# One decoder step on one core: the samples' delta rule moves into the prompt's block, its state products go between the half levels of the inverses, and its outputs are normed by token

## The reference, cut to what matters

```python
def step(S, xs):                      # per head; for a sample: one chunk of 8 tokens, S from the input
    v_new = u_c - w_c @ S             # u, w come from the inverse of (I + A), A strictly lower triangular
    o = (q_c * exp(gc_c)) @ S + att_c @ v_new
    S = S * exp(g_last) + (k_c * exp(g_last - gc_c)).T @ v_new
...
o = o * rsqrt(mean(o * o, -1) + RMS_EPS) * norm_g * silu(z)
y = o.reshape(B, L, H_DN * DV) @ w_out
```

## Time and profile before

| | |
|---|---|
| Median of 3 executions | 1855.16 us (1853.79 to 1858.89) |
| Profiled execution: time, span of its instructions | 1858.92 us, 1857.1 us |
| Last prompt chunk, from its first matmul to the first of the samples' block | 379.01 to 404.37 us |
| Samples' block, from its first matmul to the first of the next block | 404.37 to 469.92 us |
| TensorE busy, share of the span | 96% |

### The profile page before, as it was taken

The page is one execution under the profiler, slowest core; times in us unless marked ns, Lnnn a source line. Parts: engine busy times, 40 slices in busy tenths (PEclk is TensorE's granted clock), DMA queues, the critical chain, the costliest instruction groups (busy, mean ns, idle before and its releaser), DMA issues. The chain is left out here.

```text
span 1857.1 us, 22145 instructions
## 1 busy us (share of the span) xinstructions
PE 1787.9 (96%) x7791; PEld 1389.3 (75%) x7791; DVE 1153.9 (62%) x2240; ACT 454.9 (24%) x1084; POOL 279.5 (15%) x569
## 2 busy tenths in 40 slices
PE   7999999999889999999999999999899999999999
PEld 5677678997557777777777777777577777777767
DVE  3756578885776676666334665556777666653365
ACT  1433413552132222221002311111322222200041
POOL 0111102645141000000112000002310000001120
PEclk9999999997999999999999999999899999999999
DMA  4222211021212222224113032220122222322211
GB/s 167 68 69 68 64 35 46 1 99 60 92 46 69 71 88 68 81 78 146 68 58 113 1 126 88 80 81 4 63 70 84 76 80 80 108 103 94 80 48 51
DMA packets 44318, 138.05 MB, mean 74 GB/s; under 512 B 4776, under 2 KB 12072, under 8 KB 44080
## 3 DMA queue, kind: packets, MB, share of 16 engines
q1 hardware_dynamic: 41504, 132.90, 21.6%
q10 hardware_dynamic: 2704, 3.74, 0.6%
HBM read 128.32 MB, written 8.29 MB: 74 GB/s over the span
## 5 line engine op out<-in xcount | busy, mean ns | idle before, releaser
L267 PE MATMUL bank<-z,ring 128*128 128x288 f32 x1952 | 512.0, 410 | 7.0 <-DVE z L365 2.9
L267 PEld LDWEIGHTS bank<-z,ring 128*128 128x128 f32 x1952 | 373.6, 192 | 115.2 <-issue 3.2
L267 PE MATMUL bank<-x,ring 128*128 128x288 f32 x1632 | 432.3, 412 | 10.3 <-DMA x<-in_x 6.3
L267 PEld LDWEIGHTS bank<-x,ring 128*128 128x128 f32 x1632 | 313.8, 193 | 103.5 <-issue 13.4
L267 PE MATMUL bank<-y,ring 128*128 128x288 f32 x616 | 160.7, 413 | 5.9 <-DVE x L1692 3.7
L1943 DVE SCALAR_TENSOR_TENSOR scratch<-scratch 128x592 f32<-128x592 f32 x176 | 146.3, 832 | 25.6 <-ACT scratch L1887 24.0
L267 PEld LDWEIGHTS bank<-y,ring 128*128 128x128 f32 x616 | 118.3, 193 | 41.8 <-issue 5.5
L267 PE MATMUL bank<-big,ring 128*128 128x288 f32 x536 | 137.7, 412 | 7.2 <-issue 5.0
L267 PEld LDWEIGHTS bank<-big,ring 128*128 128x128 f32 x536 | 103.1, 193 | 38.6 <-issue 10.2
L1977 POOL COPY scratch<-scratch 128x2 f32<-128x2 f32 x88 | 26.6, 302 | 465.7 <-ACT scratch L1873 465.7
L1887 ACT ACTIVATE scratch<-scratch 128x592 f32<-128x592 f32 x88 | 69.4, 789 | 90.9 <-DVE scratch L1917 89.3
(11 more groups left out here) (356 smaller groups left out, 2510.2 us busy)
## 6 DMA issues: line engine op xcount, KB each, us to landing
ring<-in_w_up SPq DMA_DIRECT2D x88, 512.0 KB, 3.5
ring<-in_w_qkv SPq DMA_DIRECT2D x24, 512.0 KB, 3.5
ring<-in_w_scin SPq DMA_DIRECT2D x24, 512.0 KB, 3.5
ring<-in_w_down SPq DMA_DIRECT2D x12, 704.0 KB, 4.1
scratch<-in_w_down SPq DMA_DIRECT2D x12, 704.0 KB, 4.7
ring<-in_w_z SPq DMA_DIRECT2D x8, 512.0 KB, 3.5
big<-in_st_S SPq DMA_DIRECT2D x16, 256.0 KB, 6.4
out_dn_S_sample<-big SPq DMA_DIRECT2D x16, 256.0 KB, 2.0
```

What stands on the lines that cost most here:

```text
L267: last = pe.matmul(bank[:, 0:HALF], w[:, k * P:(k + 1) * P], rhs(k), start=start and k == 0, stop=k == self.depth - 1, skip_group_check=no ...
```

## The change

`delta_sample` and `SampleNorm` go; a class `Samples` takes their place, and its parts are appended to the prompt's block on each engine.

- **Set-up beside the last chunk.** ACT's exponentials and POOL's mask addition, clearing of the windows (now three slots), first three heads' windows, start of `T` and a clearing in `Y` run in the last chunk of the prompt. The states of a head are loaded when its last prompt product is done. k and v are turned right behind the products with k.
- **State products between half levels.** Heads 0 and 1 in level 0, heads 2 and 3 in level 1, heads 4 and 5 in level 2: one product between `y` and `d`, one after `d`. Heads 6 and 7 follow the gate of the prompt's last outputs, which now takes four heads at a time in banks 6 and 7.
- **Outputs by token.** The part of q and the states stays in PSUM and the rest is accumulated on it. ACT copies and squares each head's outputs, POOL computes the root and scales (`scale_pool`), TensorE turns them at the end, and DVE gates them from PSUM.
- The decayed values of r=1 go to `Z`, which POOL clears after the gate. POOL multiplies four states by their decays before that.
- In the next block, `SampleNorm` and the wait on it are gone.

```diff
                         for h in range(H):
                             act.activation(DEC[1 - c % 2][:, h, :], DEC[1 - c % 2][:, h, :], ACT.Exp,
                                            bias=TOKS[:, c + 1, 0, h:h + 1]).then_inc(self.dec, 1)
+                    else:
+                        samples.prepare_act(act)
                     for h in range(H):
                         act.wait_ge(self.ymask, n2 + H + h)
                         act.activation(KTOK[:, h, :], BANK[h][:, CH:2 * CH], ACT.Copy,
@@ -615,10 +617,10 @@
                     for h in range(H):
                         act.wait_ge(self.s_out, n + h)
                         act.activation(OT[:, h, :], BANK[h][:, 256:384], ACT.Copy)
...
+            def order(self, lv):
+
+
+                first = FILL[2 * lv:2 * lv + 2]
+                return first + [h for h in range(H) if h not in first]
...
+            def outputs_pe(self, pe, h):
+
+
+                pe.wait_ge(self.vn, h + 1)
+                pe.matmul(BANK[h][:, P:2 * P], S_KA[A, h, :, :], S_VNEW[A, h, :], start=False, stop=True,
+                          skip_group_check=True).then_inc(self.o, 1)
+
+            def update_pe(self, pe, h, r):
+                if r:
+                    pe.wait_ge(self.vb1, h + 1)
+                    pe.wait_ge(self.s_out, updates(h, 0))
+                else:
+                    pe.wait_ge(self.vb0, h + 1)
+                    pe.wait_ge(self.o_sq, h + 1)
+                if h == 0:
+                    pe.wait_ge(self.pad, 2 + r)
+                pe.matmul(BANK[h][:, :], S_KTOK[:, h, :], decayed(h, r), start=True, stop=True).then_inc(self.su, 1)
+
...
+            def pe(self, pe):
+                for h in range(H):
...
+                    pe.transpose(BANK[h][A, P:2 * P], smp(3 * h + 2), IDENT[:]).then_inc(self.kq, 1)
+                pe.wait_ge(self.init, 1)
+                for lv in range(SAMP_LEVELS):
+                    first, second = FILL[2 * lv:2 * lv + 2]
+                    for h in self.order(lv):
+                        if lv:
+                            pe.wait_ge(self.t, self.nth(lv - 1, h))
+                        else:
+                            pe.wait_ge(self.tok, 2 * h + 2)
+                        pe.matmul(BANK[h][A, 0:SAMP], S_KA[A, h, 0, :], S_T[A, h, 0, :], start=True,
+                                  stop=True).then_inc(self.y, 1)
+                    pe.wait_ge(self.ymask, self.nth(lv, first))
+                    self.states_pe(pe, first)
+                    for h in self.order(lv):
+                        pe.wait_ge(self.ymask, self.nth(lv, h))
+                        pe.matmul(BANK[h][A, 256:320], S_T[A, h, 1, :], S_YS[A, h, :], start=True, stop=True)
+                        pe.matmul(BANK[h][A, 320:384], S_YS[A, h, :], S_T[A, h, 1, :], start=True,
+                                  stop=True).then_inc(self.d, 1)
+                    pe.wait_ge(self.t, self.nth(lv, second))
+                    self.states_pe(pe, second)
+                pe.wait_ge(self.prompt.scaled, NCH)
+                first, second = range(GROUP), range(GROUP, H)
+                for group in range(2):
+                    pe.wait_ge(self.t, self.nth(SAMP_LEVELS - 1, 6 + group))
+                    for n in range(GROUP):
+                        last = pe.transpose(BANK[6 + group][:, n * P:(n + 1) * P], OT[:, group * GROUP + n, :], IDENT[:])
+                    last.then_inc(self.turned, 1)
+                for h in first:
+                    self.values_pe(pe, h)
+                pe.wait_ge(self.prompt.gated, (NCH - 1) * H + 1)
+                self.states_pe(pe, 6)
+                pe.wait_ge(self.prompt.gated, (NCH - 1) * H + 2)
+                self.states_pe(pe, 7)
+                for h in first:
+                    self.outputs_pe(pe, h)
+                for h in second:
+                    self.values_pe(pe, h)
+                for h in first:
+                    self.update_pe(pe, h, 0)
+                for h in second:
+                    self.outputs_pe(pe, h)
+                for h in first:
+                    self.update_pe(pe, h, 1)
+                for h in second:
+                    self.update_pe(pe, h, 0)
+                for h in first:
+                    self.turn_pe(pe, h)
+                for h in second:
+                    self.update_pe(pe, h, 1)
+                for h in second:
+                    self.turn_pe(pe, h)
+
...
+            def dve(self, dve):
+                for h in range(H):
...
+                for lv in range(SAMP_LEVELS):
+                    for n, h in enumerate(self.order(lv)):
+                        dve.wait_ge(self.y, lv * H + n + 1)
+                        if lv and h == FILL[2 * lv - 1]:
+                            self.right_side_dve(dve, h)
+                        dve.scalar_tensor_tensor(out=S_YS[A, h, :], in0=BANK[h][A, 0:SAMP],
+                                                 scalar=TOKS[A, NCH, 1, h:h + 1], in1=MASKL[A, lv, A],
+                                                 op0=ALU.mult, op1=ALU.mult).then_inc(self.ymask, 1)
+                    for n, h in enumerate(self.order(lv)):
+                        dve.wait_ge(self.d, lv * H + n + 1)
+                        if h == FILL[2 * lv]:
+                            self.right_side_dve(dve, h)
+                        if lv:
+                            dve.wait_ge(self.t, self.nth(lv - 1, h))
+                        dve.tensor_tensor(S_T[A, h], S_T[A, h], BANK[h][A, 256:384].rearrange("p (a b) -> p a b", a=2),
+                                          ALU.subtract).then_inc(self.t, 1)
+                for group in range(2):
+                    dve.wait_ge(self.turned, group + 1)
+                    heads, cols = slice(group * GROUP, (group + 1) * GROUP), slice(SEQ - CH, SEQ)
+                    dve.scalar_tensor_tensor(out=BIG[:, 1:QKV_T:3, cols][:, heads], scalar=norm_g,
+                                             in0=BANK[6 + group][:].rearrange("p (h t) -> p h t", h=GROUP),
+                                             in1=Z[:, heads, cols], op0=ALU.mult, op1=ALU.mult
+                                             ).then_inc(self.prompt.gated, 1)
+                first, second = range(GROUP), range(GROUP, H)
+                for h in range(FILL[-1], H):
+                    self.right_side_dve(dve, h)
+                for h in first:
+                    self.values_dve(dve, h)
+                for h in first:
+                    self.update_dve(dve, h, 0)
+                for h in second:
+                    self.values_dve(dve, h)
+                for h in first:
+                    self.update_dve(dve, h, 1)
+                for h in second:
+                    self.update_dve(dve, h, 0)
+                for h in first:
+                    self.gate_dve(dve, h)
+                for h in second:
+                    self.update_dve(dve, h, 1)
+                for h in second:
+                    self.gate_dve(dve, h)
+
...
+            def prepare_act(self, act):
+
+
+                act.activation(S_EG, Y[:, :, SEQ:TOK], ACT.Exp).then_inc(self.eg, 1)
+                act.wait_ge(self.arg, 1)
+                for h in range(H):
+                    act.activation(S_DEC[A, h, :], S_DEC[A, h, :], ACT.Exp, bias=TOKS[A, NCH, 0, h:h + 1]
+                                   ).then_inc(self.dec, 1)
...
+            def decayed_act(self, act, h):
+                act.wait_ge(self.vn, h + 1)
+                act.wait_ge(self.prompt.gated, (NCH - 1) * H + 2)
+                for b in range(SH, NB):
+                    last = act.activation(decayed(h, 1)[A, b - SH, :], S_VNEW[A, h, :], ACT.Copy,
+                                          scale=S_DEC[A, h, NS * b + NS - 1:NS * b + NS])
+                last.then_inc(self.vb1, 1)
+
+            def outputs_act(self, act, h):
+                act.wait_ge(self.o, h + 1)
+                act.activation(S_OS[B, h, :], BANK[h][B, P:2 * P], ACT.Copy)
+                act.activation(VTOK[B, h, :], BANK[h][B, P:2 * P], ACT.Square, accum_out=SS_S[:, h:h + 1]
+                               ).then_inc(self.o_sq, 1)
...
+            def act(self, act):
+                for h in range(H):
+                    act.wait_ge(self.att, h + 1)
+                    act.activation(S_KTOK[A, h, :], BANK[h][A, 0:P], ACT.Copy).then_inc(self.tok, 1)
+                    act.activation(S_VTOK[A, h, :], BANK[h][A, P:2 * P], ACT.Copy, scale=TOKS[A, NCH, 1, h:h + 1]
+                                   ).then_inc(self.tok, 1)
+                for group in (range(GROUP), range(GROUP, H)):
+                    for h in group:
+                        self.values_act(act, h)
+                    for h in group:
+                        self.outputs_act(act, h)
+                    for h in group:
+                        self.decayed_act(act, h)
+
+
+            def select_pool(self, pool, h):
+                if h >= SLOT_N:
+                    pool.wait_ge(self.ks, h - SLOT_N + 1)
```

(82 more changed lines are left out.)

401 lines of the change are left out of this document (104 added, 297 removed).

## The result

The changed kernel takes 1836.46 us (median of 4 executions, 1835.93 to 1836.82) against 1854.47 (4 executions, 1852.31 to 1858.89) for the kernel before on the same chip: ratio 0.9903, 95% interval 0.9885 to 0.992, so 18.0 us faster. The forecast was 1834, with a range of 1829 to 1847. The profiled execution took 1836.61 us for a span of 1834.8.

The account below looks back on a forecast made before the run. TensorE, busy 96% of the span, was taken as the bound, held up in the samples' block. Tail 15.9, clock -1.7, next block 4.8 and 2.0 sum to 21.0 us off 1855.16: 1834, range 1829 to 1847.

Parts of the forecast that it names:

- p1 to p7: Next block's products: DVE's token sums start sooner without the norm, so p7 comes 4.8 us sooner after p1.
- clock behind p7: Next block: a shorter hole before p7 may not drop TensorE's clock; 2.0 us taken, 3.1 at most.
- Set-up: Before the levels: products of k, then 16 transposes at 0.12 us, 3.8 us to the first level; gain 2.0 us.
- Levels and products: Three levels with two state products each: 6.5 us a level, 19.5 in all; gain 10.4 us, set-up included.
- Heads 6 and 7, gates: After the levels: turned outputs 0.9 us, two gates about 0.75 each; products of heads 6 and 7 end at about 431.4.
- The tail: End of the samples' block: POOL's 23.4 us chain sets the end at 453.1 against 468.96; gain 15.9 us.
- Next block: After the samples: token sums 4.8 us sooner, and 2.0 us for the clock held behind the hole before p7.
- Clock: Samples' block: half of one half-clock stretch of 3.3 us assumed, a loss of 1.7 us.
- B: Clock falls between the products: half the levels at half clock gives 1842 us, all of them 1852; chance 0.20.
- C: Tail: each of eight decayed values (0.68 us) blocks POOL for its length, 5.4 us longer, 1839.6 us; chance 0.12.
- D: POOL's windows come late for heads 5 to 7, up to 5.1 us in all, 1839 us; chance 0.05.
- E: Half clock through the whole samples' part: 17 us slower than before, 1872 us; chance 0.03.

Follow-up runs that it names:

- products-apart run: Changed kernel with the state products of heads 0 to 5 moved back behind the three levels: 1835.08 us, ratio 0.9909.
- late set-up: Changed kernel with ACT's and POOL's preparations moved behind the last chunk's squares: 1840.66 us; with state products also behind the levels: 1846.76 us.
- early: Changed kernel with POOL's second decays of the first group moved ahead of its wait for the gate: 1835.62 us, ratio 0.9907.
- split: As early, plus three quarters of Z cleared in the last chunk and the second group's first decays before the first scaling: 1835.48 us.
- both late runs: The two changed kernels with preparations behind the last chunk, state products between half levels (1840.66 us) or behind the levels (1846.76 us).
- without the norm: Kernel before, with the norm and gate of the samples' outputs left out of the next block: 1842.15 us, ratio 0.9951.
- all: Changed kernel with the edits of split and of the batched run together: 1836.41 us, ratio 0.9922.
- batched run: Changed kernel with all heads' products of k first in the set-up, then the 16 transposes: 1837.84 us, ratio 0.9924.

## Why the prediction came out right, step by step

| step | forecast gain, us | measured in the two profiles |
|---|---|---|
| meeting before the samples' part | 1.3 | 1.3 |
| block, clock included | 15.9 - 1.7 - 1.3 = 12.9 | 10.1 |
| p1 to p7 | 4.8 | 4.85 |
| clock behind p7 | 2.0 | 2.95 |
| elsewhere | 0 | 3.1 |
| sum | 21.0 | 22.3 by spans; 18.0 by medians |

**What bounds it.** Right as a reading of the time, wrong in one cause. That dense 64-wide work makes the clock fall is refuted by the products-apart run. The trace of before already held the alternative: its levels followed a meeting (1.26 us idle) and a set-up in which TensorE waited another 0.78 us for DVE:

```profile
407.08 0.30 PE L1433 MATMUL bank<-identity,big 128*64 128x128 f32 x1 [0.78 <-DVE scratch L1344]
```

With a hole of 2.1 us ahead, the same levels fell to half clock after 2.0 us. That the two shorter holes did it in the kernel before is argued and not shown, since no run takes away these alone. What was right is that 64-wide work doesn't bring the clock back and that it comes back with the products.

**Set-up.** The gain of 2.0 was mis-sized: first product to first level took 5.62 us, not 3.8. The first level starts 29.65 us after the chunk's first matmul and not 29.93, so 0.3 us were gained, the meeting included. The term that failed is "16 transposes at 0.12": 0.23 us a head for changing between product and transpose was missing. That the preparation hides in the last chunk was right, to 0.1 us, and its worth was underrated: it saves the hole of 2.1 us and also the clock behind it, 4.7 us in all with products between.

**Levels and products.** 21.28 us instead of 19.5. A level takes 7.30 us at first and then 7.04, since bare it takes 3.1 and not 2.8 us and a product between half levels 2.05 and not 1.88. And the idea of the step, that overlap is the gain, is wrong: at full clock it is worth nothing. Put against the products-apart run, the 10.2 us of block come from these differences: levels at full clock 14.76 - 9.76 = 5.0; turned outputs and the way to the products 1.77 - 0.90 = 0.9; six products 11.29 - 10.88 = 0.4; from their end to the next block 33.2 - 28.2 = 5.0; less 1.0 for the longer set-up. Beside the 5.0 of the levels stands what the late set-up cost them, 14.03 - 9.76 = 4.3. No run divides the 5.0 behind the products: the norm by token, the new order of the tail and the clock (the mix near 443 at 0.53, updates of 5.37 us for 3.70) lie in them together.

**Heads 6 and 7, gates.** 2.05 us from the turning to the second gate's end, forecast 2.0.

**The tail.** The order was right: POOL without gaps from `Z` to the last decay, the last addition behind it. The chain took 24.45 us for 23.4. `scale_pool` was shorter than 3.2 (2.7 and 2.4, the power being 1.01 us for four columns), the first two groups of decays longer: 1.35 and 1.47 us each, 1.02 in the last. What I called a lead of only 1.3 us over TensorE's and ACT's chain was that in fact: the early and split runs took POOL's part away and gained 1.1 us each, early before the 1.7 us that its clock took back. The signs in absolute time came later than said, with the set-up and the levels: the products of heads 6 and 7 ended at 436.5 and not near 433, and the last gate 54.9 us after the chunk's end and not some 50.

**Next block.** Both terms right, the second at its upper end. That the clock held behind the 1.98 us hole was in part luck: in both late runs it fell behind the same hole.

**Clock.** 1.7 us were charged and nothing was paid. This, the 0.95 us more behind p7 and the 3.1 us elsewhere, which no step had forecast, make up for the 4.7 us that set-up, levels and POOL's chain were short. So the time came out near the forecast partly by luck: errors of both signs cancelled.

**Rivals.** B did not come, though for another reason than the one given. C came in part: beside each other DVE's decayed value takes 1.38 for 0.62 us and POOL's decay 1.35 to 1.47 for 1.02. In rival C each decayed value adds DVE's whole 0.68 us to POOL, 5.4 in all; eight decays grew by (5.41 + 5.90) - 8 x 1.02 = 3.2 us. The 5.4 is what the rule of the Trainium skill (SBUF — State Buffer, "Who interferes with whom"), that the two engines exclude each other for such operations, would give here as an estimate, and the trace agrees in direction only. This is slowing of both, more than my 0.2 and less than exclusion. D did not come: no wait on a window stands in the trace. E did not.

**The rest** of the medians' difference, 21.0 forecast and 18.0 measured, is within what single profiles say: the profile of before was taken in the slowest of its four executions. The 15.9 us of the tail were counted from its block, of which 1.7 us were that execution's clock near 443.

## What to carry to other kernels

Work that fills another engine's wait is worth what TensorE idles there: look for the hole before interleaving, since here interleaving had a price of its own, 0.8 us. A stage of short dependent products should be entered from dense work without a hole, because once the clock had fallen here they did not bring it back; moving some 10 us of POOL's preparation beside the previous stage was worth more than the overlap that the change was built around. When the engine that ends a tail is relieved, ask which engine ends 1 us earlier: taking POOL's work away gave 1.1 us until ACT's order was changed too.

## What the runs showed of the hardware

- Dense 64x64x64 products ran 9.76 us at a clock of 1.00 with no hole ahead. Behind a hole of 2.1 us they ran 2.0 us at 1.00 and then 11.7 us at 0.50, without bringing the clock back.
- The clock came back in or right behind 128-row products: 3.3 us after their start with the set-up late and products apart, 4.2 us with them between, 0.9 us in the kernel before (5.0, 4.2 and 2.7 us after the first 128-row work, turned outputs included).
- The same hole ahead of the same work was followed by half clock in some profiles and not in others: 0.98 us near 442 in the kernel before, but not 0.99 without the norm; 1.26 us ahead of the second group's outputs in products apart, but not 1.25 with the set-up late as well; 1.78 us there in early and all, but not 1.77 in split; 0.85 us at p1 in the batched run, but not in the changed kernel; 1.98 us at p7 in the two late runs, but not in the changed kernel. What decides is not settled.
- Four decayed values on DVE (64x512, both operands in SBUF) took 0.62 us each with POOL idle and 1.38 beside its decays; a decay of POOL (128x512) took 1.02 us alone and 1.35 to 1.47 beside them.
- A change between product and transpose on TensorE cost 0.23 us a head; a state product took 2.05 us between half levels and 1.81 in a row.
- Executions of one kernel differ by where the clock falls: thirteen of the kernel before ranged from 1843.79 us at a mean clock of 0.993 to 1858.79 at 0.982.
